# Where the first turn of a batch loop begins, which input-projection tiles its turns hold, and when the value gathers are issued

## What is computed

```python
h = rms_norm(x, g_norm1) * (1.0 + sc1) + sh1
proj = h @ w_in
q, k, v, glu_a, glu_b, gate_a, gate_c = jnp.split(proj, [A, 2 * A, 3 * A, 3 * A + C, 3 * A + 2 * C, 3 * A + 2 * C + D], axis=-1)
...
attn = moba_attention(q, k_all, v_all, pos0, alibi_slopes()) @ w_attn_proj
u = glu_a * jax.nn.sigmoid(glu_b)
conv_in = jnp.concatenate([conv_past, u], axis=1)
cv = depthwise_causal_conv(conv_in, w_dwconv) + b_dwconv
cv = jax.nn.silu(layer_norm(cv, g_conv_ln, b_conv_ln)) @ w_conv_proj
mix = (jax.nn.sigmoid(gate_a) * attn + jax.nn.sigmoid(gate_c) * cv) @ w_out
x = x + gt1 * mix
h2 = rms_norm(x, g_norm2) * (1.0 + sc2) + sh2
f_g, f_u = jnp.split(h2 @ w_ffn_in, 2, axis=-1)
x = x + gt2 * ((jax.nn.silu(f_g) * f_u) @ w_ffn_out)
```

## Time and profile before

| | us |
|---|---|
| Three timed runs | 584.61, 574.83, 580.37; median 580.37 |
| The profiled execution: time | 578.59 |
| The profiled execution: span of the trace | 576.8 |
| First sum of page scores (turn 0 begins) | 105.24 |
| Same sum in turn 7 | 283.10 |
| First product of the convolution's projection (the turns are over) | 301.91 |

### The profile page before, as it was taken

How to read it: one execution, slowest core, us unless ns; L and a number is a source line. 1 busy time by engine, 2 the same in 40 slices (tenths; PEclk the granted TensorE clock), 3 DMA queues, 4 the chain that set the end, 5 groups by cost and what they waited for, 6 DMA issues and landing times.

```text
span 576.8 us, 10394 instructions
## 1 busy us (share of the span) xinstructions
PE 517.8 (90%) x4166; PEld 438.7 (76%) x4166; DVE 396.4 (69%) x609; ACT 292.1 (51%) x519; POOL 170.1 (29%) x232
## 2 busy tenths in 40 slices
PE   4769899887989888798879999699999999999997
PEld 3558678764655646465539999699999999999996
DVE  0733584689999999989766885867666656555441
ACT  3225344587767878755463543383444444433431
POOL 8408368288677787751100000000000000000000
PEclk9679899999989999899969999989999999999999
DMA  8998639698999999999967969695665466376501
GB/s 304 371 376 329 236 145 374 249 322 298 413 390 399 410 406 411 383 391 357 402 271 275 386 240 376 234 347 190 203 215 168 147 188 160 101 201 176 149 14 39
DMA packets 82128, 159.31 MB, mean 276 GB/s; under 512 B 2573, under 2 KB 61113, under 8 KB 76952
## 3 DMA queue, kind: packets, MB, share of 16 engines
q1 hardware_dynamic: 76256, 89.27, 46.5%
q0 software_dynamic: 5120, 67.71, 29.4%
q10 hardware_dynamic: 703, 1.67, 0.8%
HBM read 156.39 MB, written 2.72 MB: 276 GB/s over the span
## 4 chain that ended last, share of the span: by engine, by line
PE 54%; DVE 23%; DMA 12%; issue 4%; ACT 4%; POOL 2%; ACTq 1%; SPq 0%; DVEq 0%; POOLq 0%
PE acc L1581 11%; PE acc L1582 11%; PE acc L1583 11%; DVE prod L1051 7%; DMA wring<-in_w_in 5%; DVE sall L1058 4%; PE acc L1453 4%; DMA wring<-in_w_ada 4%; DMA wring<-in_w_ffn_in 2%; PE acc L1466 2%; DVE wlo L1123 2%; PE acc L1467 2%; PE acc L1468 2%; PE chain L1605 2%; ACT L618 1%
## 5 line engine op out<-in xcount | busy, mean ns | idle before, releaser
L1123 DVE TENSOR_TENSOR wlo<-wring,whi 128x1024 fp32r<-128x1024 f32 (+2 forms) x84 | 92.0, 1097 | 72.7 <-ACT whi L618 71.7
L618 ACT ACTIVATE whi<-wring 128x1024 fp32r<-128x1024 f32 (+2 forms) x84 | 80.0, 958 | 81.3 <-PE acc L1583 74.1
L1581 PE MATMUL acc<-xlo,whi 128*128 128x264 f32 x384 | 110.1, 287 | 0.2
L1582 PE MATMUL acc<-xhi,wlo 128*128 128x264 f32 x384 | 108.8, 283 | 0.0
L1583 PE MATMUL acc<-xhi,whi 128*128 128x264 f32 x384 | 108.8, 283 | 0.0
L573 POOL TENSOR_TENSOR cvT<-cvT,cprod 128x256 f32<-128x256 f32 x120 | 87.7, 731 | 43.3 <-ACT cprod L618 28.4
L1453 PE MATMUL acc<-hT,wring 128*128 128x264 f32 x336 | 92.3, 419 | 3.8 <-DVE hT L1011 2.0
L1453 PEld LDWEIGHTS acc<-hT,wring 128*128 128x128 f32 x336 | 64.1, 202 | 18.0 <-issue 5.4
L1581 PEld LDWEIGHTS acc<-xlo,whi 128*128 128x128 f32 x384 | 72.3, 188 | 1.3 <-issue 0.9
L1058 DVE TENSOR_REDUCE sall<-prod 128x32 f32<-128x2048 f32 x32 | 73.0, 2281 | 0.4
L1582 PEld LDWEIGHTS acc<-xhi,wlo 128*128 128x128 f32 x384 | 72.4, 189 | 0.0
(11 more groups left out here) (317 smaller groups left out, 906.9 us busy)
## 6 DMA issues: line engine op xcount, KB each, us to landing
wring<-in_w_ada SPq DMA_DIRECT2D x22, 1024.0 KB, 9.7
wring<-in_w_ffn_in SPq DMA_DIRECT2D x22, 1024.0 KB, 7.7
wring<-in_w_in SPq DMA_DIRECT2D x12, 1024.0 KB, 10.4
wring<-in_w_ffn_out SPq DMA_DIRECT2D x16, 704.0 KB, 5.6
more<-in_w_out SPq DMA_DIRECT2D x4, 1024.0 KB, 11.0
wring<-in_w_in SPq DMA_DIRECT2D x6, 512.0 KB, 20.4
wring<-in_w_in SPq DMA_DIRECT2D x4, 768.0 KB, 20.7
wring<-in_w_conv_proj SPq DMA_DIRECT2D x2, 1024.0 KB, 11.2
```

Of the source, the lines that this page charges most:

```text
L618: return nc.scalar.activation(out, in_, f, **kw)
L1123: v.tensor_tensor(wlo[:, place, 0:n, :], w, whi[:, place, 0:n, :].bitcast(F32), ALU.subtract)\
L1581: mm(bank[:, 0:R], whi[:, place, k - k0, :], lo[:, k, :], start=k == 0, stop=False)
L1582: mm(bank[:, 0:R], wlo[:, place, k - k0, :], hi[:, k, :], start=False, stop=False)
```

## The change

- Turn 0 now begins right behind the value units and the key norms. The split tiles a0 and b0 and the value transposes move into it: a0 ahead of the mask, b0 around `spread_max`, the value rows behind it (`values_to_rows`), a1 around `spread_sum`.
- b1 is no longer split: it is a plain tile and the third of turn 0. All later tiles follow in the order `TURN_TILES`; the gates stand a turn later, and turn 7 holds g14 and g15, with g13's two halves around its start.
- ACT reads a0 behind the prompt's exponential in turn 0, b0 behind the scaled probabilities, and copies and stores keys and values in two parts, `keys_out` at the turn's start and `values_out` behind the exponential of the scores.
- DVE makes the first gated product ahead of the exponentials' sum, the second one in turn 1.
- POOL issues the first value gather behind v0's rest, a key gather more (`gather_k(5)`) ahead of the loop, and the second value gather when a1 is done. It waited for b1 there.
- The convolution has 10 taps in turn 0 and 22 (7, 7, 8) in turns 1 to 5, where it had 20 in each of turns 0 to 5.

```diff
-THIRD = {0: "a2", 1: "b2", 2: "a3", 3: "b3", 4: "g10", 5: "g13"}
-FIRST_GATE = (0, 2, 4, 6, 8, 11, 14)
+TURN_TILES = (("b0", "a1", "b1"), ("a2", "a3", "b2"), ("b3", "g0", "g1"), ("g2", "g3", "g4"), ("g5", "g6", "g7"),
+              ("g8", "g9", "g10"), ("g11", "g12", "g13"), ("g14", "g15"))
...
+         + ["ks", "kn0", "kn1", "so", "a0", "b0", "vn0", "vn1", "vs", "a1", "b1"])
+for _b in range(1, B):
+    FILLS.append(TURN_TILES[_b][0])
     if _b == B - 2:
         FILLS += ["ct", "lnm"]
-    FILLS.append(f"g{FIRST_GATE[_b] + 1}")
-    FILLS.append(THIRD.get(_b, "lnv"))
+    FILLS.append(TURN_TILES[_b][1])
+    if _b == B - 2:
+        FILLS.append("lnv")
+    if _b < B - 1:
+        FILLS.append(TURN_TILES[_b][2])
...
-CONV_PART = CT * (TAPS - 1) // CONV_LOOPS
-CONV_SPLIT = (6, 6, 8)
+CONV_PARTS = ((0, 0, 10),) + ((7, 7, 8),) * (CONV_LOOPS - 1)
...
                     gather_k(2)
+                    gather_v(0, 0)
                 if name == "v2":
                     gather_k(3)
-                if name == "v3":
-                    gather_v(0, 0)
-                if name == "b1":
+                if name == "a1":
                     gather_k(4)
+                    gather_k(5)
...
-                    pool.wait_ge(acc_full, NUMBER["b1"] + 1)
+                    pool.wait_ge(acc_full, NUMBER["a1"] + 1)
                     gather_v(0, 1)
                 else:
                     for c in range(CH):
                         gather_v(b, c)
                 add_taps(b, 1)
-                gather_k(CH * b + 5)
+                if b > 0:
+                    gather_k(CH * b + 5)
...
+            def values_out():
+
+                for name, dst in (("vn0", vnat[:, 0, :]), ("vn1", vnat[:, 1, :])):
+                    rows_out(name, dst)
+                bank = when_full(act, "vs")
+                freed(func(vrow, bank[32:32 + B, :], ACT.Copy), "vs")
+                for name in ("vn0", "vn1", "vs"):
+                    wait_freed(act, name)
+                for t in range(2):
+                    act.dma_start(v_prompt[0, t * P:(t + 1) * P].rearrange("p h d -> p (h d)"), vnat[:, t, :])\
+                        .then_inc(stored, 16)
+                act.dma_start(v_sample.rearrange("b o h d -> b (o h d)"), vrow).then_inc(stored, 16)
...
-                    glu("a", 1)
+                    keys_out()
+                    bank = when_full(act, "so")
+                    freed(func(sown[:, :, :].rearrange("p b h -> p (b h)"), bank[:, 0:B * H], ACT.Copy), "so")
...
+                    tile_out("a0")
+                else:
+                    tile_out(TURN_TILES[b - 1][2])
...
+                tile_out(TURN_TILES[b][0])
                 act.wait_ge(s2_ready, b + 1)
                 func(s1[:, :, :], s1[:, :, :], ACT.Exp).then_inc(e_ready, 1)
+                if b == 0:
+                    values_out()
...
-                    gated_glu(0)
-                    dve.wait_ge(u_ready, 1)
...
-                if j == 0 and 0 < i < CT - 1:
-                    gated_glu(i + 1)
+                if b in (1, 2, 4):
+                    gated_glu(1 + b // 2)
...
                 add_up_next(2)
+                if b == 0:
+                    dve.wait_ge(consts, 3)
+                    gated_glu(0)
+                    dve.wait_ge(u_ready, 1)
                 dve.wait_ge(e_ready, b + 1)
...
+            def third(b, k0, k1):
+
+                w, t = (slot_ready("glu"), 3) if b == 0 else (slot_ready(f"mix{b - 1}"), 2)
+                tile(TURN_TILES[b][2], w, t, hT, k0=k0, k1=k1)
...
-                    split("a1")
-
-                if b - 1 in THIRD:
-                    tile(THIRD[b - 1], mix, 2, hT, k0=4, k1=7)
+                    split("a0")
+
+                if b >= 1:
+                    third(b - 1, 4, 7)
...
-                    split("b1")
+                if b >= 1:
+                    third(b - 1, 7, KD)
 
                 pe.wait_ge(m1_ready, b + 1)
                 nc.tensor.transpose(turned_, m1, ident[:, :]).then_inc(m1t_ready, 1)
-                if b < B - 1:
-                    mix, first = slot_ready(f"mix{b}"), FIRST_GATE[b]
-                    tile(f"g{first}", mix, 0, hT, k1=4)
+                if b == 0:
+                    split("b0", k1=4)
+                else:
+                    mix = slot_ready(f"mix{b - 1}")
+                    tile(TURN_TILES[b][0], mix, 0, hT, k1=4)
...
-                if b < B - 1:
-                    tile(f"g{first}", mix, 0, hT, k0=4)
+                if b == 0:
+                    split("b0", k0=4)
+                    values_to_rows()
+                else:
+                    tile(TURN_TILES[b][0], mix, 0, hT, k0=4)
 
...
+                    split("a1", k1=5)
+                else:
+                    tile(TURN_TILES[b][1], mix, 1, hT, k1=5)
...
-                if b in THIRD:
-                    tile(THIRD[b], mix, 2, hT, k1=4)
+                if b < B - 1:
+                    third(b, 0, 4)
```

113 lines of the change are left out of this document (49 added, 64 removed).

## The result

The changed kernel took 588.89 us (median of four runs, 584.12 to 593.77), the kernel before 581.38 us (four runs, 574.83 to 584.61): ratio 1.016, 95% interval 1.011 to 1.022. The predicted 583 was 6 us too low; the time lies inside the range of 572 to 593. It is slower, by an amount at the border of what I called no change.

The account below looks back on a forecast made before the run. DVE was taken to set the pace in turns 1 to 6, with PE's order counting at both ends. Terms -6.4 - 2.0 + 6.4 + 0 + 5.6 + 0 = +3.6 us gave 582.2 to 584.0, stated as 583, range 572 to 593.

Parts of the forecast that it names:

- What bounds the kernel: Turns 1 to 6: DVE sets the pace, busy 24.1 to 24.4 us of turns lasting 24.9 to 25.5.
- Term 1: Start of turn 0: split tiles and value transposes no longer precede the page scores' sum on PE, 6.4 us earlier.
- Term 2: Turn 0: DVE's wait for the exponential is filled and the second gated product moves to turn 1, 2.0 us shorter.
- Term 3: Turn 1: 6.4 us given back, as the second value gather waits for a1 and DVE stalls for the gate.
- Both chains of the step: Turn 1: late value gather delaying the gate (4.7 us stall); POOL's tap additions delaying ACT's copy `pvm` to near 136.
- Term 4: Turns 2 to 6: no change, PE's tiles and POOL's 22 additions still fit; 0, between -1 and +4 us.
- Term 5: Turn 7: g13's halves, g14 and g15 delay attention steps, partly offset by a full clock (-1.8); 5.6 us longer.
- A: Turn 7's tiles fit PE's waits and only the start counts: 572 to 580 us, chance 0.22.
- B: PE stays at 1.2 GHz in turn 7 through g13's second half, g14 and g15: up to +17, 594 to 596, chance 0.09.
- C: Value gather landing at 14.9 us and one weight load at 27: +5.5 and +2, near 590, chance 0.08.
- D: Turn 0's start does not move because key norms slip, so -6.4 is missing: about 587 us, chance 0.05.

Follow-up runs that it names:

- the run with parts 5, 8, 9: Changed kernel with its 22 convolution taps of turns 1 to 5 cut 5, 8, 9 instead of 7, 7, 8: 581.91 us, ratio 1.004.
- parts 4, 8, 8: Kernel before with its 20 convolution taps a turn cut 4, 8, 8 instead of 6, 6, 8: 580.05 us, ratio 0.995.
- the a1 run: Changed kernel with a1 as a plain tile, so the second value gather and turn 0's taps wait for b0: 582.51 us, ratio 1.005.
- the small parts: Changed kernel with a1 plain, taps 8 in turn 0; 2, 9, 9 in turn 1; 5, 7, 8 in turns 2-5; later store wait: 583.43 us, ratio 0.993.

## Why the prediction was right and where it was wrong

- **What bounds the kernel.** Right: DVE's 24 us per turn are the floor. Whatever was repaired, turns came back to 24.1 to 25.1; the shortest in any trace is 23.4.
- **Term 1, start of turn 0, -6.4.** -3.3 in the profiled execution, -4.1 in the second. The step "from the end of the value rows to the sum of scores PE needs 1.4" took its durations at full clock. They ran at the lower level, and so did the last key norms. DVE ended these at 99.2 for 97.3, and the copy came 3.2 us behind them, where it takes 1.9 in the run with parts 5, 8, 9. There the clock held until the norms were done, and the gain was there: the copy at 97.9 is 7.7 us earlier than before, of which 1.3 are older than the change (first norms at 88.85 for 90.12). The 6.4 that are left are the forecast. Why the clock falls a little earlier or later is open. The kernel before is not safe either: with parts 4, 8, 8 its stretch 92 to 100 had 0.50 and turn 0 began at 108.3.
- **Term 2, turn 0, -2.0.** -1.7.
- **Term 3, turn 1, +6.4.** +8.0. From the first multiply to the masked scores the turn is 8.4 us longer, forecast 6.6, and behind them 0.3 shorter, forecast 0.2. The mis-sized step is the one from `pvm` to the masked scores, 3.7 us, which took 5.5 at a granted clock of 0.73 and 0.67. Also, the second half of the weighing took 3.34 us, not half of 3.62, so DVE's wait for the gate was 6.24, not 4.7. Both chains of the step were real, as the a1 run and the small parts show one after the other: 33.5, 30.2, 25.0.
- **Term 4, "turns 2 to 6: nothing".** This is the step that failed: +8.2 in turns 2 to 5, by far the largest miss. (The "twenty-odd plain half tiles" of that step are steps: three tiles of eight.) It summed POOL's work, "22 x 0.86 + 4 gathers x 0.96 = 22.8 us of 24.9, tight but inside". The sum was right (POOL is busy for 19.3 to 20.2 us, and its pitch is 0.87), but the limit is not in the sum. One more addition stands in the chain from the start of part 2 to a copy on which the mask depends. I had worked out this very chain for turn 1 and did not ask it of turns 2 to 5. The late copy is just covered as long as PE has its full clock (24.1 to 24.6 us), and it tips the turn when the clock is lower. Counted over all profiled executions: with seven taps in part 0, 16 of 20 turns 2 to 5 lasted 25.3 us or more, 13 of them without a wait for weights; with five or six, in the changed order, 5 of 24, each with such a wait. In the turns without a wait for weights, the clock was 0.81 to 0.87 in 12 of 17 with seven taps and never under 0.93 in the 19 with five or six. So the longer chain goes with the lower clock; how it brings it about is not shown. The range of that step, -1 to +4, was too narrow by half.
- **Term 5, the last turn, +5.6.** +3.9, the 0.9 by which the sum of scores comes late (DVE's wait for it 1.38 against 0.48) being in turn 6 of the table. Counted from the copy of turn 7, before and after: masked scores 7.07 and 7.53, exponential 10.18 and 14.44, last weighing 13.10 and 17.88, the convolution's first product 18.39 and 21.43. With the 0.9 the exponential is 5.2 late (forecast 5.6) and the weighing 5.7 (forecast 7.4). The mis-sized step is the one from the exponential to the weighing, "about 0.5 over, and the last three eighths of g15": it adds 0.5, not 1.8. The clock came as forecast:

```profile
310.00 0.32 ACT L628 ACTIVATE s<-s 128x136 f32<-128x136 f32 x1
313.44 3.62 PE L1624 MATMUL chain<-vring,pg 128*8 128x512 f32 x32
```

  3.62 us where the earlier trace rows had 5.36. Leaving g14 and g15 out gave back only 1.1 us, since the weighing then took 5.87.
- **Rivals.** A (the ends are free) fell: turn 7 did cost. B (a lower clock in turn 7) fell: it was granted in full there, and low in turns 1 to 5 instead (0.81 to 0.90). C (late transfers) is real, but as scatter from one execution to the next, in both kernels; PE waited for no weight load in turns 1 to 6 of the changed kernel's two profiled executions. D (the start does not move) is half true, the norms did slip.
- **Luck.** 588.89 lies in the stated range, but just outside the forecast's own 578 to 588 and close to C's 590, for a reason that neither of them has. The wide range carried it.

The terms that missed are +3.1, +1.6, +8.2 and -1.7, with +0.3 of turn 0 and +0.1 behind the turns: 11.6 us, the difference between +15.2 and +3.6.

What stays open is the clock. The late copy does not come from it, since `pvm` was 2.9 us behind DVE's copy at 0.81 and at 1.00 alike. But the same wait of 1.4 us for it stood in turns at 1.00, so what makes the clock fall in one turn and not in the next is not known. No run has the short chain at a clock of 0.81 without a wait for weights, so the part of the low clock alone is not separated. Nor is it known how much of the 8.2 us the medians would show: both profiled executions of the changed kernel were among its longest.

## What to carry to other kernels

Where two engines pass work through a short ring, the sum of the work says nothing of the handoff behind it. Find the point where the slower engine last stands idle, count the items from there to the step that others wait for, at its pace, and do so in every turn, not only in the one that the change is about. Here the items of the part before counted as much as those next to the copy. When a change lengthens turns that it should not touch, look first at tables that spread side work over them: two more taps per turn, one of them in this chain, cost 6.6 us in the kernel before without any reordering. And once the turns are tight against full DMA engines, a removed wait may not show in the median, so compare many runs.
